# A Strassen-like down projection: places of the weight tiles, order of the first tile's parts, output additions, squares' sums

## The chip, the cores and the metric

One Trainium2 chip; the kernel runs on 1 core. The metric is the device time of that core in microseconds (us). The core has TensorE (PE, matmuls), VectorE (DVE), ScalarE (ACT), GpSimd (POOL) and SyncE (SP), which in this kernel issues all loads and stores; 16 DMA engines carry them out. The engines run each its own list of instructions in order and wait for each other on semaphores.

## The reference

One layer of a decoder, for 1024 prompt tokens and 64 sample tokens (1088 columns in the kernel), in float32. The change touches only its last lines:

```
    x = x + merged @ w_out
    h2 = rmsnorm(x, norm2_g)
    x = x + (jax.nn.silu(h2 @ w_gate) * (h2 @ w_up)) @ w_down
    return x, c_kv, k_r, v
...
    y_prompt = rmsnorm(xp, final_norm_g)
    y_sample = rmsnorm(xs, final_norm_g)
```

D_MODEL is 1024, D_FF 2816 (22 tiles of 128). Everything ahead of it (attention, gMLP, output projection) is the same instructions in both kernels.

## The kernel before

**Tiling.** Activations lie transposed: features on the 128 partitions, tokens along the free side. A product of a float32 operand pair is made of three matmuls of parts (`mm3`, L893 to L895): a *high* part, made by ACT as a rounded copy (L1474), and a *low* part, the rest, made by DVE as a subtraction. The MLP is not computed as one matmul: rows, columns and the sum index are each halved, and seven products of sums of the halves (M2, M6, M4, M1, M3, M5, M7 in this order) take the place of eight. `TURNS` is 11, `RING` is 4.

**Gate and up.** 11 turns of 7 products (j from 0 to 6, 6.0 us each on TensorE). ACT and POOL make the parts of the weights (`cw_hi`, `cw_lo`), DVE collects the results in `bufP`, `bufC` and `bufD` (L2442, semaphore `added`), ACT applies silu (L1805), DVE multiplies (`times`, L2489, semaphore `blocks`), and SP stores the four finished blocks in DRAM (`acts`, L592).

**Down.** 88 steps t: product p = t // 11, tile k = t % 11. In the first six products a step has 24 matmuls with 272 columns. The seventh (M7) is done in two halves of the columns, with 12 matmuls a step: t from `LAST` = 66 to 76, and from `LATE` = 77 to 87. For each step:

- SP (`load_down`) loads one or two blocks of `w_down` of 256 KB into place `t % RING` of `araw` (three blocks for M3, of which one goes to `a7` and stays for M7), and (`load_tile`) a tile of the activations into `ab[1]`, `ab[2]`, `ab[3]`. It also brings back the rows of x (`x<-x2s`). `load_down(t)` waits for the low part of the weights of tile t - 4, so SP follows DVE. `ab[0]` comes in two transfers (`load_ab0`): ten tiles in one (2720 KB), and the last tile alone.
- DVE sums the weight blocks (`down_sum`, L2567, L2571), sums the activation tiles (`act_sum`, L2584), and makes the low parts (`down_low`: `aHL` for the weights, L2592, and `bHL` for the activations, L2595). ACT makes the high parts (`down_high`, `act_high`) into rings of four.
- TensorE waits for `dn_lo` and adds into 8 PSUM banks. At a product's end ACT copies them to `part` (`keep_product`, at the third step of the next product, semaphore `dn_ev`), and DVE adds or subtracts `part` to one or two blocks of x2 (`add_parts`, L2605, at the fourth step, semaphore `y_add`). A block is 4 row tiles by half of the tokens. M7 goes from PSUM to x2 directly (`add_last`).

The order of DVE's instructions in one step t of the down projection is: `down_sum(t)`, `act_sum(t)`, `down_low(t - 1)`, then `add_parts`, then the extra work of the last steps.

**The last turn of gate and up** mixes both stages. The four places of `araw` are the same memory as the four places of `wraw` that hold gate and up weights. They come free in the order 0, 2, 3, 1 (`cw_lo` 1, 5, 6, 7 of the turn), and the loads of tile 0, 2, 3, 1 are issued at these points. `ab[0]` lies where operands of the first products lay, and is issued behind tile 3:

```
                sp_.wait_ge(cw_lo, PROD * i + 6)
                if last:
                    load_down(3)
                    load_ab0(0, TURNS - 1)
```

On ACT, `down_high(0)`, `act_high(0)` and `down_high(1)` stand behind `silu(i, bufC[:, 0, :], 11)`. On DVE, `down_sum(0)` and `down_sum(1)` stand ahead of the last additions (`block21`), `down_low(0)` stands between the second product of `bufC` and `block12`, `down_low(1)` behind `block12`.

**The final norm** is made for three groups of columns (`COLUMNS`: 544, 272, 272). ACT squares the blocks of x2 as they become final (`sqy`, `sqh`, `sqt`), DVE folds them (L2617, semaphore `n5_add`), TensorE sums over the partitions (`token_sums`, L1405), DVE makes means (L2624), POOL the power -1/2 (L885), DVE diagonals (L2632), TensorE spreads them over the partitions (`token_spread`, L1420), ACT copies that to `rs5`, and DVE scales (L1956). The first group's sums stand on TensorE ahead of step 73 (`LAST + 7`), its spread ahead of step 75 (`LAST + 9`); step 77 needs `rs5`. The folds of `sqy`, which belong to the second and third group, stand at step 70; those of `sqh` at 72 and 74.

Of the kernel before, what the change touches and what calls it, by code (L numbers as in the profile page):

```python
# [32 lines left out]
KD = D // P  # L33
# [56 lines left out]
           M3: ((1, 1), (3, 1)), M5: ((0, -1), (1, 1)), M7: ((0, 1),)}  # L90
STEPS = (PROD + 1) * TURNS
RING = 4
LAST, LATE = STEPS - 2 * TURNS, STEPS - TURNS
# [42 lines left out]
def build(nc, d):  # L136
    ctx = ExitStack()
    with ctx:
# [234 lines left out]
        ab_full = [sem(f"ab_full{b}") for b in range(4)]  # L373
        a_sum, b_sum, dn_hi, dn_lo = (sem(n) for n in ("a_sum", "b_sum", "dn_hi", "dn_lo"))
# [56 lines left out]
        def w_down(t):  # L431
            return a7[:, t % TURNS, :] if t >= LAST else araw[:, t % RING, 0, :]
# [39 lines left out]
        def _(sp_):  # L472
# [121 lines left out]
            def turn(i, last=False):  # L594
# [9 lines left out]
                if last:  # L604
                    load_down(2)
# [11 lines left out]
                if last:  # L617
                    load_down(1)
# [8 lines left out]
            def load_ab0(k0, k1):  # L627
# [4 lines left out]
                sp_.dma_start(ab[0][:, k0:k1, :], acts[0, k0:k1, :, :].rearrange("t p n -> p t n")).then_inc(ab_full[0], 16)  # L632
# [11 lines left out]
            def load_down(t):  # L644
# [3 lines left out]
                for x, (a, _) in enumerate(A_TERMS[p]):  # L648
                    sp_.dma_start(araw[:, t % RING, x, :], d["w_dn"][a, k, :, :]).then_inc(ff_full[t % RING], 16)
                if p == M3:  # L650
# [4 lines left out]
                    sp_.dma_start(a7[:, k, :], d["w_dn"][1, k, :, :]).then_inc(ff_full[t % RING], 16)  # L655
                    sp_.dma_start(araw[:, t % RING, 1, :], d["w_dn"][3, k, :, :]).then_inc(ff_full[t % RING], 16)
# [233 lines left out]
        def _(pe):  # L890
# [565 lines left out]
            pe.wait_ge(n5_add, 2)  # L1456
# [15 lines left out]
        def _(act):  # L1472
# [368 lines left out]
            def down_high(t):  # L1841
# [13 lines left out]
                else:  # L1855
                    act.wait_ge(ff_full[t % RING], raw_loads(t))
# [27 lines left out]
            def turn(i, par, last=False):  # L1884
# [8 lines left out]
                silu(i, bufC[:, 0, :], 11)  # L1893
# [4 lines left out]
                else:  # L1898
# [25 lines left out]
            for t in range(2, STEPS):  # L1924
# [12 lines left out]
                elif t == LAST + 5:  # L1937
                    act.wait_ge(y_add, adds_to(M7))
# [14 lines left out]
        def _(dve):  # L1953
# [581 lines left out]
            def turn(i, last=False):  # L2535
# [26 lines left out]
            def down_sum(t):  # L2562
                p, k = t // TURNS, t % TURNS
                if p < M7 and len(A_TERMS[p]) == 2:
                    dve.wait_ge(ff_full[t % RING], raw_loads(t))
                    x = araw[:, t % RING, :, :]
# [238 lines left out]
```

## Time and profile before

| | us |
|---|---|
| three timed runs | 1433.33, 1427.6, 1430.66; median 1430.66 |
| profiled execution: its time | 1435.15 |
| its span in the profile | 1433.4 |
| PE busy | 1345.6 (94%) |
| DVE busy | 834.2 (58%) |
| ACT busy | 507.9 (35%) |
| POOL busy | 427.5 (30%) |
| mean granted TensorE clock, of 2.4 GHz | 0.967 |

The page of the profile gives per engine the busy time, then the span in 40 slices, the chain of work that ended last (here 73% PE, 14% DVE), and the costliest groups of instructions. The costliest by far are the three matmul lines of the down projection (L893 to L895, 616 each, some 290 ns one). Matmuls overlap: one of 290 ns starts every 125 ns at the full clock. The down projection runs from 1168 us to 1420 us.

### The profile page before, as it was taken

Reading aid. Unit: us, or ns where it says so; the run is one execution under the profiler, and the core shown is the slowest. Engines: PE = TensorE matmul, PEld = TensorE weight load, DVE = VectorE, ACT = ScalarE, POOL = GpSimd, SP = SyncE. Lnnn points to the kernel's source line nnn. Section 1 sums busy time; section 2 is a strip of 40 time slices with the busy share of each in tenths; the row PEclk is TensorE's granted clock in tenths of the full one; section 3 lists DMA queues with packets and bytes.
Section 4 is the critical chain, followed back from the end, with each engine's and each line's share of the span. In section 5 each row is a group of like instructions: output and inputs, shape, how many; then the busy total and the mean of one; then the engine's idle time right before and its main releaser. Section 6 shows DMA issues by size and latency. Waiting matters only on the chain.

```text
span 1433.4 us, 23985 instructions
## 1 busy us (share of the span) xinstructions
PE 1345.6 (94%) x9450; PEld 1255.6 (88%) x9450; DVE 834.2 (58%) x1272; ACT 507.9 (35%) x884; POOL 427.5 (30%) x277
## 2 busy tenths in 40 slices
PE   6999997899999898999989999999999989999987
PEld 4778896788888765999989999999999989999987
DVE  4795035566665432717893444554344558989976
ACT  3413122565555422402432222222222224444451
POOL 1262232434433102566124444444444410000000
PEclk8999998899999799999999999999999999999998
DMA  7001000100005343463022212222222269857503
GB/s 237 17 30 64 31 30 12 65 1 19 1 16 176 137 138 121 165 211 102 27 83 84 81 61 75 75 82 75 82 74 77 76 226 327 285 191 237 168 1 125
DMA packets 66970, 146.33 MB, mean 102 GB/s; under 512 B 7778, under 2 KB 15330, under 8 KB 66178
## 3 DMA queue, kind: packets, MB, share of 16 engines
q1 hardware_dynamic: 66882, 145.12, 30.0%
q8 instruction: 59, 0.97, 0.3%
q14 instruction: 29, 0.24, 0.1%
HBM read 122.54 MB, written 22.55 MB: 101 GB/s over the span
## 4 chain that ended last, share of the span: by engine, by line
PE 73%; DVE 14%; issue 5%; DMA 3%; ACT 2%; POOL 1%; SPq 0%; DVEq 0%; POOLq 0%; ACTq 0%
PE ps L893 22%; PE ps L894 21%; PE ps L895 21%; DMA araw<-in_w_dn 2%; PE ps L1116 2%; PE ps L901 2%; DVE x L1956 2%; PE ps L1179 1%; DVE aHL L2592 1%; DMA x<-in_x 1%; DVE bHL L2595 1%; PE ps L1222 1%; DVE bsum L2584 1%; DVE uwL L2013 1%; DVE hL L2007 1%
## 5 line engine op out<-in xcount | busy, mean ns | idle before, releaser
L893 PE MATMUL ps<-bHL,aHL 128*128 128x272 f32 x616 | 179.9, 292 | 11.2 <-DVE bHL L2595 11.2
L862 POOL TENSOR_TENSOR ws<-wraw,ws 128x1024 fp32r<-128x1024 f32 x50 | 124.4, 2488 | 217.2 <-ACT ws L1474 217.2
L895 PE MATMUL ps<-bHL,aHL 128*128 128x272 f32 x616 | 179.1, 291 | 0.0
L894 PE MATMUL ps<-bHL,aHL 128*128 128x272 f32 x616 | 178.4, 290 | 0.0
L893 PEld LDWEIGHTS ps<-bHL,aHL 128*128 128x128 f32 x616 | 118.4, 192 | 12.8 <-DVE bHL L2595 12.7
L2442 DVE TENSOR_TENSOR bufP<-bufP,ps 128x544 f32<-128x544 f32 x66 | 47.4, 720 | 135.5 <-PE ps L895 133.2
L1474 ACT ACTIVATE ws<-wraw 128x1024 fp32r<-128x1024 f32 x55 | 58.4, 1061 | 173.5 <-PE ps L895 170.3
L895 PEld LDWEIGHTS ps<-bHL,aHL 128*128 128x128 f32 x616 | 117.9, 191 | 0.0
L894 PEld LDWEIGHTS ps<-bHL,aHL 128*128 128x128 f32 x616 | 117.7, 191 | 0.0
L2193 DVE TENSOR_TENSOR pTL<-ps,pTH 128x512 fp32r<-128x512 f32 (+1 forms) x96 | 53.1, 554 | 53.7 <-ACT pTH L1474 53.3
L885 POOL TENSOR_TENSOR rt<-ms,mhalf 128x3 f32<-128x3 f32 (+1 forms) x3 | 3.1, 1024 | 265.8 <-DVE ms L2624 265.8
L862 POOL TENSOR_TENSOR ws<-wsum,ws 128x1024 fp32r<-128x1024 f32 x20 | 58.3, 2913 | 61.8 <-ACT ws L1474 61.8
L808 POOL TENSOR_TENSOR prob<-prob,rsm 128x128 f32<-128x128 f32 (+5 forms) x48 | 49.6, 1041 | 88.5 <-DVE rsm L2168 88.5
L1474 ACT ACTIVATE aHL<-araw 128x512 fp32r<-128x512 f32 x66 | 41.6, 631 | 88.5 <-DVE araw L2567 58.0
L2442 DVE TENSOR_TENSOR bufC<-bufP,ps 128x544 f32<-128x544 f32 x42 | 30.2, 720 | 70.6 <-PE ps L895 70.6
L1474 ACT ACTIVATE pTH<-ps 128x512 fp32r<-128x512 f32 (+1 forms) x96 | 46.8, 489 | 51.4 <-PE ps L1116 50.6
L1116 PE MATMUL ps<-ident,prob 128*128 128x128 f32 x288 | 52.0, 287 | 10.7 <-DVE prob L2173 7.5
L1627 ACT ACTIVATE prob<-ps,nmx 128x128 f32<-128x128 f32 (+3 forms) x64 | 47.3, 740 | 23.2 <-DVE nmx L2179 23.2
L2179 DVE TENSOR_REDUCE nmx<-ps 128x1 f32<-128x128 f32 (+3 forms) x64 | 47.7, 750 | 12.2 <-PE ps L1097 12.1
L704 POOL TENSOR_TENSOR rt<-ms,mhalf 128x3 f32<-128x3 f32 x15 | 14.6, 976 | 134.0 <-DVE ms L1976 121.5
L893 PE MATMUL ps<-x6H,ws 128*128 128x272 f32 x176 | 51.7, 294 | 2.7 <-DVE x6L L2525 2.7
L1116 PEld LDWEIGHTS ps<-ident,prob 128*128 128x128 f32 x288 | 34.8, 146 | 19.9 <-DVE prob L2173 8.5
(362 smaller groups left out, 4640.1 us busy)
## 6 DMA issues: line engine op xcount, KB each, us to landing
araw<-in_w_dn SPq DMA_DIRECT2D x121, 256.0 KB, 3.3
wraw<-in_w_gu SPq DMA_DIRECT2D x44, 512.0 KB, 3.6
cp<-in_cache SPq DMA_DIRECT2D x64, 272.0 KB, 4.7
ab<-acts SPq DMA_DIRECT2D x34, 272.0 KB, 5.0
raw<-in_w_out SPq DMA_DIRECT2D x16, 512.0 KB, 4.4
acts<-bufC SPq DMA_DIRECT2D x22, 272.0 KB, 2.1
x<-in_x SPq DMA_DIRECT2D x4, 1088.0 KB, 7.4
x<-x2s SPq DMA_DIRECT2D x8, 544.0 KB, 6.6
```

The costliest lines, as they stand in the source:

```text
L808: pool.tensor_tensor(row, row, rsm[:, r % 4:r % 4 + 1].broadcast_to((P, n)), ALU.mult).then_inc(s_pn, 1)
L862: pool.tensor_tensor(w[:, 1, :], w_source(j), w[:, 0, :], ALU.subtract).then_inc(cw_lo, 1)
L893: nc.tensor.matmul(out, wh, xh, start=start, stop=False)
L894: nc.tensor.matmul(out, wh, xl, start=False, stop=False)
L895: return nc.tensor.matmul(out, wl, xh, start=False, stop=stop)
L901: last = nc.tensor.matmul(ps[:, bank, 0:n], ones[:, :], sq[:, kk, 0:n], start=kk == 0, stop=kk == k - 1)
L1116: last = nc.tensor.transpose(ps[:, 4 + x % 2, P * qi:P * qi + P], prob[:, at:at + P], ident[:, :])
L1474: return nc.scalar.activation(out, x, ACT.Copy, scale=scale)
L1627: nc.scalar.activation(prob[:, prob_at(qt):prob_at(qt) + n], psf[:, 1024 * (r % 2):1024 * (r % 2) + n], ACT.Exp, bias=nmx[:, s:s + 1], sca ...
L2179: nc.vector.tensor_reduce(nmx[:, s], psf[:, at:at + P * (qt + 1)], AX.X, ALU.max, negate=True).then_inc(s_nm, 1)
L2193: nc.vector.tensor_tensor(pTL[:, x % 4, c0:512], ps[:, 4 + x % 2, c0:512], pTH[:, x % 4, c0:512], ALU.subtract).then_inc(t_free, 1)
L2442: nc.vector.tensor_tensor(halves(out[:, g, :]), halves(x[:, g, :]), pair(b + 2 * g), ALU.add).then_inc(added, 1)
```

## The change

It reorders and renames; no product, load or matmul is added or taken away.

- **Places.** `SLOTS = (0, 2, 3, 1)`: tile t goes to place `SLOTS[t % 4]`. In the last turn tile 1 is loaded at the second of the four points, into place 2; tile 2 at the third, into place 3, behind the first part of `ab[0]`; tile 3 at the last, into place 1. The last tile of `ab[0]` has a semaphore of its own, `ab_last`.
- **First tile's parts.** On ACT, `down_high(0)`, `act_high(0)`, `down_high(1)` go ahead of the silu of `bufC`. On DVE, `down_low(0)` goes ahead of `block21`.
- **Additions apart.** `add_parts(p)`, which made one or two additions at the fourth step of the next product, becomes `add_part(p, x)`: the first at the fourth step, the second at the fifth. M5's targets change places, so block 1 is final first.
- **Squares' sums.** ACT squares block 1 at step 70 (was 71) after the first of M5's additions. DVE's `sqh` folds go from steps 72 and 74 to 71, 72 and 73; the `sqy` folds from step 70 to step 78, behind `token_diagonals(0)`. TensorE's waits on `n5_add` have new numbers.

```diff
-           M3: ((1, 1), (3, 1)), M5: ((0, -1), (1, 1)), M7: ((0, 1),)}
+           M3: ((1, 1), (3, 1)), M5: ((1, 1), (0, -1)), M7: ((0, 1),)}
...
+SLOTS = (0, 2, 3, 1)
...
-                engine.wait_ge(ab_full[0], 16 if k < TURNS - 1 else 32)
+                engine.wait_ge(ab_full[0] if k < TURNS - 1 else ab_last, 16)
...
-            return a7[:, t % TURNS, :] if t >= LAST else araw[:, t % RING, 0, :]
+            return a7[:, t % TURNS, :] if t >= LAST else araw[:, SLOTS[t % RING], 0, :]
...
                 sp_.wait_ge(cw_lo, PROD * i + 5)
                 if last:
-                    load_down(2)
+                    load_down(1)
...
                 sp_.wait_ge(cw_lo, PROD * i + 6)
                 if last:
-                    load_down(3)
                     load_ab0(0, TURNS - 1)
+                    load_down(2)
...
                 if last:
-                    load_down(1)
+                    load_down(3)
                     load_ab0(TURNS - 1, TURNS)
...
                 if t == LAST + 7:
-                    pe.wait_ge(n5_add, 6)
+                    pe.wait_ge(n5_add, 4)
...
-            pe.wait_ge(n5_add, 2)
+            pe.wait_ge(n5_add, 6)
...
-                silu(i, bufC[:, 0, :], 11)
                 if last:
                     down_high(0)
                     act_high(0)
                     down_high(1)
-                else:
+                silu(i, bufC[:, 0, :], 11)
+                if not last:
                     weights_high(i + 1, 0, 1 - par)
...
-                elif t == LAST + 5:
-                    act.wait_ge(y_add, adds_to(M7))
+                elif t == LAST + 4:
+                    act.wait_ge(y_add, adds_to(M5) + 1)
                     square(sqh[:, 0:KH, :], slice(0, KH), half1, n5_sq)
...
                     down_sum(0)
                     down_sum(1)
+                    down_low(0)
                 for g in range(2):
                     block21(i, g)
                 times(i, bufC, 3, 12)
-                if last:
-                    down_low(0)
...
-                if t % TURNS == RING - 1 and TURNS <= t < LATE:
-                    add_parts(t // TURNS - 1)
-                if t == LAST + 4:
-                    fold(sqy, 2, 1)
-                    dve.wait_ge(n5_add, 1)
-                    fold(sqy, 1, 1)
+                if TURNS <= t < LATE and t % TURNS in range(RING - 1, RING - 1 + len(TARGETS[t // TURNS - 1])):
+                    add_part(t // TURNS - 1, t % TURNS - RING + 1)
+                if t == LAST + 5:
+                    fold(sqh[:, KH:KD, :], 2, 2)
                 elif t == LAST + 6:
-                    fold(sqh[:, KH:KD, :], 2, 2)
-                elif t == LAST + 8:
                     fold(sqh[:, 0:KH, :], 2, 3)
-                    dve.wait_ge(n5_add, 4)
+                elif t == LAST + 7:
+                    dve.wait_ge(n5_add, 2)
                     nc.vector.tensor_tensor(sqh[:, 0:2, :], sqh[:, 0:2, :], sqh[:, KH:KH + 2, :],
                                             ALU.add).then_inc(n5_add, 1)
-                    dve.wait_ge(n5_add, 5)
+                    dve.wait_ge(n5_add, 3)
                     fold(sqh, 1, 3)
...
                 elif t == LATE + 1:
                     token_diagonals(0)
+                    fold(sqy, 2, 1)
+                    dve.wait_ge(n5_add, 5)
+                    fold(sqy, 1, 1)
```

SP's queue in the last turn, before (`araw<-in_w_dn` are weight blocks, two for a tile; `ab_173` is `ab[0]`):

```order
L592 DMA acts<-bufC 128x544
L649 DMA araw<-in_w_dn 128x512 x4
L632 DMA ab_173<-acts 128x10x544
L592 DMA acts<-bufD 128x544
L649 DMA araw<-in_w_dn 128x512 x2
L632 DMA ab_173<-acts 128x544
```

and now:

```order
L594 DMA acts<-bufC 128x544
L651 DMA araw<-in_w_dn 128x512 x2
L634 DMA ab_173<-acts 128x10x544
L651 DMA araw<-in_w_dn 128x512 x2
L594 DMA acts<-bufD 128x544
L651 DMA araw<-in_w_dn 128x512 x2
L634 DMA ab_173<-acts 128x544
```

The big transfer stands ahead of the third pair of blocks now, not behind it, and the pairs are those of tiles 1, 2, 3 instead of 2, 3, 1.

DVE in the same place, before (`aHL_183` and `bHL_177` are the parts of step 0, `aHL_184` and `bHL_178` of step 1):

```order
L2489 TENSOR_TENSOR bufD<-bufD 128x544
L2567 TENSOR_TENSOR araw<-araw 128x512 x2
L2442 TENSOR_TENSOR bufC<-bufC,ps 128x544 x2
L2489 TENSOR_TENSOR bufC<-bufC 128x544
L2592 TENSOR_TENSOR aHL_183<-araw,aHL_183 128x512
L2595 TENSOR_TENSOR bHL_177<-ab_173,bHL_177 128x544
L2442 TENSOR_TENSOR bufP<-bufP,ps 128x544 x2
```

and now:

```order
L2491 TENSOR_TENSOR bufD<-bufD 128x544
L2568 TENSOR_TENSOR araw<-araw 128x512 x2
L2593 TENSOR_TENSOR aHL_183<-araw,aHL_183 128x512
L2596 TENSOR_TENSOR bHL_177<-ab_173,bHL_177 128x544
L2444 TENSOR_TENSOR bufC<-bufC,ps 128x544 x2
L2491 TENSOR_TENSOR bufC<-bufC 128x544
L2444 TENSOR_TENSOR bufP<-bufP,ps 128x544 x2
```

Step 0's low parts moved ahead of the two additions into `bufC` and its product.

DVE in the last product, from the additions of M5 on, before (one `aHL` and one `bHL` row are a step's low parts, 69 first):

```order
L2605 TENSOR_TENSOR x_145<-x_145,part 128x4x544 x2
L2592 TENSOR_TENSOR aHL_184<-a_188,aHL_184 128x512
L2595 TENSOR_TENSOR bHL_178<-ab_174,bHL_178 128x272
L2617 TENSOR_TENSOR sqy<-sqy 128x1088
L2617 TENSOR_TENSOR sqy<-sqy 128x544
L2592 TENSOR_TENSOR aHL_194<-a_188,aHL_194 128x512
L2595 TENSOR_TENSOR bHL_179<-ab_174,bHL_179 128x272
L2592 TENSOR_TENSOR aHL_195<-a_188,aHL_195 128x512
L2595 TENSOR_TENSOR bHL_180<-ab_174,bHL_180 128x272
L2617 TENSOR_TENSOR sqh<-sqh 128x1088
```

and now:

```order
L2606 TENSOR_TENSOR x_145<-x_145,part 128x4x544
L2593 TENSOR_TENSOR aHL_184<-a_188,aHL_184 128x512
L2596 TENSOR_TENSOR bHL_178<-ab_174,bHL_178 128x272
L2606 TENSOR_TENSOR x_145<-x_145,part 128x4x544
L2593 TENSOR_TENSOR aHL_194<-a_188,aHL_194 128x512
L2596 TENSOR_TENSOR bHL_179<-ab_174,bHL_179 128x272
L2618 TENSOR_TENSOR sqh<-sqh 128x1088
L2593 TENSOR_TENSOR aHL_195<-a_188,aHL_195 128x512
L2596 TENSOR_TENSOR bHL_180<-ab_174,bHL_180 128x272
L2618 TENSOR_TENSOR sqh<-sqh 128x1088
```

The second addition stands behind step 69's low parts, the two `sqy` folds are gone from here, and each `sqh` fold comes a step or two earlier.

## Rows read from the trace of the kernel before

**Rows 1.** The page, busy time by engine: us, share, instructions

```profile
PE 1345.6 (94%) x9450; PEld 1255.6 (88%) x9450; DVE 834.2 (58%) x1272; ACT 507.9 (35%) x884; POOL 427.5 (30%) x277
```

**Rows 2.** Waits of TensorE, 1140 to 1434: waited for, us, times, longest

```profile
PE ps L893 <- DVE bHL L2595: 11.2, 7, 4.7
```

**Rows 3.** Timeline, the start: start, us, engine, line, [idle before <- releaser]

```profile
1150.27 0.39 SPq L632 DMA_DIRECT2D ab<-acts  x1
...
1164.40 0.69 DVE L2567 TENSOR_TENSOR araw<-araw 128x512 f32<-128x512 f32 x1 [7.46 <-DMA araw<-in_w_dn]
...
1166.84 0.64 ACT L1474 ACTIVATE bHL<-ab 128x544 fp32r<-128x544 f32 x1
...
1167.70 0.72 DVE L2595 TENSOR_TENSOR bHL<-ab,bHL 128x544 fp32r<-128x544 f32 x1
...
1168.47 0.60 PE L893 MATMUL ps<-bHL,aHL 128*128 128x272 f32 x1 [4.66 <-DVE bHL L2595]
...
1170.96 0.72 DVE L2489 TENSOR_TENSOR bufP<-bufP 128x544 f32<-128x544 f32 x1
...
1172.10 0.92 SPq L649 DMA_DIRECT2D araw<-in_w_dn  x2
```

**Rows 4.** The loads of `ab[0]`, line L632: time from issue to landing

```profile
DMA to landing us min/median/max: 7.0/8.9/10.9
```

**Rows 5.** Stretches: length, busy us of each engine (count), PEclk, DMA share, GB/s

```profile
1164.00:1168.40 4.40, 0.00 (x0) 0.00 (x0) 3.90 (x7) 2.24 (x4) 0.00 (x0) 0.87 0.08 34
1168.40:1174.00 5.60, 5.53 (x24) 5.53 (x25) 5.40 (x10) 2.83 (x6) 0.00 (x0) 0.50 0.26 94
1186.00:1192.00 6.00, 6.00 (x50) 6.00 (x49) 4.22 (x7) 2.36 (x4) 0.00 (x0) 1.00 1.05 401
1377.00:1382.00 5.00, 1.92 (x14) 1.55 (x12) 4.96 (x7) 4.38 (x8) 0.00 (x0) 1.00 0.00 0
1390.00:1394.00 4.00, 4.00 (x19) 4.00 (x20) 2.46 (x7) 0.00 (x0) 1.17 (x1) 0.50 0.00 0
```

**Rows 6.** Timeline, first product: step 1, two low parts, eviction, step 11

```profile
1174.08 0.29 PE L893 MATMUL ps<-bHL,aHL 128*128 128x272 f32 x1
...
1177.11 0.72 DVE L2595 TENSOR_TENSOR bHL<-ab,bHL 128x544 fp32r<-128x544 f32 x1
...
1180.47 0.72 DVE L2595 TENSOR_TENSOR bHL<-ab,bHL 128x544 fp32r<-128x544 f32 x1
...
1204.76 2.15 ACT L1474 ACTIVATE part<-ps 128x544 f32<-128x544 f32 x4
...
1205.51 0.36 PE L893 MATMUL ps<-bHL,aHL 128*128 128x272 f32 x1 [1.40 <-DVE bHL L2595]
```

**Rows 7.** Timeline: the first pair of additions, steps 14 and 47 on TensorE

```profile
1207.80 4.97 DVE L2605 TENSOR_TENSOR x<-x,part 128x2176 f32<-128x2176 f32 x2
...
1215.30 0.39 PE L893 MATMUL ps<-bHL,aHL 128*128 128x272 f32 x1 [0.59 <-DVE bHL L2595]
...
1315.62 0.39 PE L893 MATMUL ps<-bHL,aHL 128*128 128x272 f32 x1 [0.59 <-DVE bHL L2595]
```

**Rows 8.** Timeline, last product: additions, step 69, fold, token sums, power, diagonals, spread

```profile
1373.33 4.99 DVE L2605 TENSOR_TENSOR x<-x,part 128x2176 f32<-128x2176 f32 x2 [1.94 <-ACT part L1474]
...
1379.32 0.39 PE L893 MATMUL ps<-bHL,aHL 128*128 128x272 f32 x1 [2.16 <-DVE bHL L2595]
...
1386.16 1.28 DVE L2617 TENSOR_TENSOR sqh<-sqh 128x1088 f32<-128x1088 f32 x1
...
1389.58 2.29 PE L1405 MATMUL ps<-ones,sqh 128*128 128x1 f32 x10 [2.47 <-DVE sqh L2617]
...
1392.54 1.17 POOL L885 TENSOR_TENSOR rt<-ms,mhalf 128x5 f32<-128x5 f32 x1 [237.17 <-DVE ms L2624]
...
1395.66 0.82 DVE L2632 TENSOR_TENSOR diag<-ident,rt 128x640 f32<-128x640 f32 x1
...
1396.70 1.85 PE L1420 MATMUL ps<-diag,ones 128*128 128x128 f32 x16
```

More of the change, by code:

```diff
@@ L373, in build @@
         ab_full = [sem(f"ab_full{b}") for b in range(4)]
+        ab_last = sem("ab_last")
         a_sum, b_sum, dn_hi, dn_lo = (sem(n) for n in ("a_sum", "b_sum", "dn_hi", "dn_lo"))
@@ L631, in load_ab0 @@
                 sp_.wait_ge(act_out[0], 16 * k1)
-                sp_.dma_start(ab[0][:, k0:k1, :], acts[0, k0:k1, :, :].rearrange("t p n -> p t n")).then_inc(ab_full[0], 16)
+                sp_.dma_start(ab[0][:, k0:k1, :], acts[0, k0:k1, :, :].rearrange("t p n -> p t n")).then_inc(ab_full[0] if k0 == 0 else ab_last, 16)
             def load_tile(b, k):
@@ L654, in load_down @@
                         sp_.wait_ge(dn_lo, 2 * TURNS * M1)
-                    sp_.dma_start(a7[:, k, :], d["w_dn"][1, k, :, :]).then_inc(ff_full[t % RING], 16)
-                    sp_.dma_start(araw[:, t % RING, 1, :], d["w_dn"][3, k, :, :]).then_inc(ff_full[t % RING], 16)
+                    sp_.dma_start(a7[:, k, :], d["w_dn"][1, k, :, :]).then_inc(ff_full[SLOTS[t % RING]], 16)
+                    sp_.dma_start(araw[:, SLOTS[t % RING], 1, :], d["w_dn"][3, k, :, :]).then_inc(ff_full[SLOTS[t % RING]], 16)
             turn(0)
@@ L1855, in down_high @@
                 else:
-                    act.wait_ge(ff_full[t % RING], raw_loads(t))
+                    act.wait_ge(ff_full[SLOTS[t % RING]], raw_loads(t))
                 hi(weights_of(t)[:, 0, :], w_down(t)).then_inc(dn_hi, 1)
@@ L2564, in down_sum @@
                 if p < M7 and len(A_TERMS[p]) == 2:
-                    dve.wait_ge(ff_full[t % RING], raw_loads(t))
-                    x = araw[:, t % RING, :, :]
+                    dve.wait_ge(ff_full[SLOTS[t % RING]], raw_loads(t))
+                    x = araw[:, SLOTS[t % RING], :, :]
                     nc.vector.tensor_tensor(x[:, 0, :], x[:, 0, :], x[:, 1, :],
@@ L2569, in down_sum @@
                 elif p == M3:
-                    dve.wait_ge(ff_full[t % RING], raw_loads(t))
-                    nc.vector.tensor_tensor(a7[:, k, :], a7[:, k, :], araw[:, t % RING, 1, :],
+                    dve.wait_ge(ff_full[SLOTS[t % RING]], raw_loads(t))
+                    nc.vector.tensor_tensor(a7[:, k, :], a7[:, k, :], araw[:, SLOTS[t % RING], 1, :],
                                             ALU.subtract).then_inc(a_sum, 1)
@@ L2595, in down_low, with add_part @@
                 nc.vector.tensor_tensor(x[:, 1, :], act_of(t), x[:, 0, :], ALU.subtract).then_inc(dn_lo, 1)
-            def add_parts(p):
+            def add_part(p, x):
+                b, sign = TARGETS[p][x]
                 dve.wait_ge(dn_ev, KH * (p + 1))
-                for x, (b, sign) in enumerate(TARGETS[p]):
-                    for j in range(2):
-                        dve.wait_ge(ld_x[2 * (b // 2) + j], 64)
-                    if adds_to(p) + x:
-                        dve.wait_ge(y_add, adds_to(p) + x)
-                    nc.vector.tensor_tensor(y_block(b), y_block(b), part[:, :, :],
-                                            ALU.add if sign > 0 else ALU.subtract).then_inc(y_add, 1)
+                for j in range(2):
+                    dve.wait_ge(ld_x[2 * (b // 2) + j], 64)
+                if adds_to(p) + x:
+                    dve.wait_ge(y_add, adds_to(p) + x)
+                nc.vector.tensor_tensor(y_block(b), y_block(b), part[:, :, :],
+                                        ALU.add if sign > 0 else ALU.subtract).then_inc(y_add, 1)
             with dve.Fori(0, (TURNS - 3) // 2) as i:
```

2 lines of the change are left out of this document (1 added, 1 removed).

## The prediction

> **What bounds the kernel now.** I first read the page's engine lines: TensorE's matmuls are busy for 94% of the span [rows 1], so only places where TensorE stops, or runs at its lower clock, can give time. Next, the waits of TensorE in the down projection [rows 2]: 11.2 us in 7 waits, all for DVE's L2595, the low part of an activation operand. The timeline says where they lie and which of them the change touches. A *step* below is one tile t of the down projection; step t cannot start before `down_low(t)` has made both low parts. A full step takes 2.99 us at the full clock, a step of the last product (t from 66 on) 1.5 us (24 and 12 matmuls of about 0.125 us).
>
> Three places count. (a) Step 0 starts at 1168.47 after 4.66 us of idleness, that is, the gate and up stage ended at 1163.8 [rows 3]. Then the granted clock is 0.50, the 1.2 GHz level, until step 1 begins at 1174.08 [rows 5, 6]: 5.6 us instead of 3.0. (b) Steps 14 and 47 start 0.59 us late each, behind DVE's pairs of output additions [rows 7]. (c) In the last product step 69 starts 2.16 us late, step 70 again late, the token sums 2.47 us late and then at the lower clock [rows 5, 8].
>
> **Place a: the start.** DVE sat 7.46 us in `down_sum(1)` until the second tile's two weight blocks landed, at 1164.40 [rows 3]. Those are issued last of the first four tiles, behind the 2720 KB load of `ab[0]`. With the change tile 1 goes to the place that tile 2 had, two gate and up products (12 us) earlier; the 7.46 us go. What is late next? `down_low(0)` needs `ab[0]`, issued at 1150.27 and landed 10.9 us later, at 1161.2 [rows 3, 4]. The new order issues it ahead of two 256 KB blocks instead of behind them: 0.85 us earlier (two issues), and with 0.52 MB less ahead of it, 1.3 us at the 401 GB/s of [rows 5]. So it lands between 1159.0 (both) and 1161.2 (neither). I take 1160.0.
>
> Here one rule of the Trainium skill bears on the choice. "DMA: Bandwidth & Descriptors", under "Queues, rings and completion order", says that each DMA engine takes descriptors in ring order, while completion is not first in, first out. By the first half alone the landing would be 1159.0, by the second it could stay at 1161.2. No row here shows a transfer of this size behind another and also ahead of it.
>
> From a landing at 1160.0 the rest is a chain of known pieces: ACT's high part 0.64, DVE's low part 0.72, two bufC additions, the product, two bufP additions, again low part and product, each of 128x544 and 0.72 or less like the rows of [rows 3], with ACT's silus, of the size of a high part, beside or between them. It has `down_low(0)` ready at 1161.4, before TensorE is free at 1163.8, so step 0 starts at 1163.85, without idleness and without the lower clock. Step 1 is ready at 1166.2 (wanted at 1166.85), the last product of the block (row 1170.96 of [rows 3]) ends at 1166.9, and SP, whose next tile load is queued behind that product's store, issues `load_down(4)` at 1167.35 instead of 1172.10: 4.75 us earlier. With the landing at 1161.2 it is 3.55; with 1159.0, where the last gate and up matmul at 1163.8 becomes the limit, 5.15.
>
> Now the important cut. TensorE would be 7.2 us earlier at step 1 (1174.08 to 1166.85), but it doesn't keep that. In the first product the weight blocks, the `ab[1]` tiles and the returning rows of x keep the DMA engines full: 401 GB/s [rows 5], and `down_low(4)` followed `down_low(3)` by 3.36 us (1177.11 to 1180.47, [rows 6]), not by 2.99. Before, TensorE's late and slow step 0 covered that: `down_low(3)` ended at 1177.83 and step 3 was wanted only at 1180.06 (1174.08 and two steps). Now the feed moves by 4.75 and TensorE by 7.2, so steps 3 to 7 wait 0.2 to 0.5 us each. At step 11 the feed sets the time already: ACT evicts the first product only after `act_high(13)`, at 1204.76, and step 11 starts at 1205.51 [rows 6]. That whole chain moves with SP's first issue. **Term a: 4.75 us (3.55 to 5.15; 7.2 if the feed should catch up).**
>
> **Place b: additions apart.** Two additions of 2.45 us each (4.97 together) sit between `down_low(13)` and `down_low(14)` [rows 7]. Apart, the second goes behind `down_low(14)`: step 14 loses its 0.59 us and the start-up 0.1; `down_low(15)`, behind both, ends as before, about 0.1 us later than TensorE now wants it. Gain 0.6. At step 47 the same pattern gives 0.6 (there `down_low(48)` becomes 0.15 late). The pairs at steps 36 and 58 held nobody up and are worth nothing; DVE's total work there is unchanged, so the short wait at step 44, whose low parts come late by a wait of SP's, stays. **Term b: 1.2 us (0.7 to 1.5).**
>
> **Place c: the last product.** DVE's additions start at 1373.33, TensorE ends step 68 at 1377.15 [rows 8]. In the new order: addition 1 ends at 1375.8, step 69's low parts at 1376.8 (they take 1.0 us: 1378.32 to 1379.32), in time; 2.16 us saved. Addition 2 to 1379.2, step 70 ready at 1380.15 (1.6 late), fold 1.28 us and low parts: step 71 ready at 1382.3 (0.6 late), fold and low parts: step 72 at 1384.4 (0.6 late), the joining addition 1.28 and the half-size fold 0.7: token sums at 1386.4 instead of 1389.58. Taking the sqy folds, 2.0 us, out ahead of the sums is part of this. Gain so far 3.2. ACT's square of block 1 comes 2 us earlier in its queue, ahead of the highs of step 71; those end at 1379.7 and are wanted at 1381.3, so they cost nothing. The ten matmuls of the sums ran at the 0.50 clock [rows 5]; at the full clock they take 1.15 instead of 2.29. Then comes a part that gives something back: the mean is read by DVE only after the low parts of steps 73 to 76 (4 by 0.95: 1390.1; before, the sums themselves came last), the power takes 1.17 us on POOL, the diagonals 0.82, and the spread before step 75 starts at 1392.45 instead of 1396.70 [rows 8], after some 1.9 us of idleness. The sqy folds now follow the diagonals; TensorE has steps 75 and 76 in stock and DVE is through at 1394.4, 2.8 us before the first addition from step 76 needs it: free. Everything behind (second token sums, last scaling, stores of y) hangs on TensorE's end and moves along. **Term c: 4.25 us (2.3 if the lower clock is no part of a usual execution, up to 4.6).**
>
> The semaphore `ab_last`, one more DVE instruction per pair and the sign order of M5 cost nothing that a row shows: they lie on engines with idle time there.
>
> **Sum.** 4.75 + 1.2 + 4.25 = 10.2 us. The profiled execution took 1435.15 us, so it would take 1424.95. It lies 4.5 us above the median of the three runs; I take the difference off the median: 1430.66 - 10.2 = 1420.5.
>
> **Rivals.**
> 1. *The lower clock was a thing of the profiled execution.* TensorE idled 3.1 of the 5.0 us from 1377 to 1382 and stayed at the full clock, and lost it some 5 us later, after 2.47 idle us [rows 5, 8]. If the timed executions mostly keep it, the sums' 1.15 and step 73's 1.36 us weren't there to win: term c about 2.2, the time 1422.5. Speaks for it: the timed runs are all faster than the profiled one.
> 2. *The feed doesn't move.* If the DMA engines deliver the first product's tiles no earlier (a slower stretch, or `ab[0]` 1 to 2 us later than 1161.2), term a falls to 0 to 1.5 and the time is about 1425.5. Against it: they are nearly idle from 1164 to 1174, 34 and 94 GB/s [rows 5], and only SP's wait keeps them so.
> 3. *New waits lower the clock.* The idle stretches are 1.6, 0.6, 0.6, 0.4 and 1.9 us in the last product, and one drop there costs about 2.6 us: 1423.
> 4. *Slower than before.* The mechanism is the same clock in the starved steps 3 to 7: a step at the lower level costs 2.6 us more (5.61 against 2.99). Four such steps eat the whole gain; seven, with the half steps of the last product at 1.36 each, make it slower by over 0.5%, about 1439. Against it: these waits are under 0.5 us of each 3.4, and 3.1 idle us of 5.0 left the clock at 1.00 [rows 5].
>
> The Trainium skill's rule speaks for 3 and 4: "TensorE: Matmul & The Clock Gate" holds the slow level for the default which activity releases, and its section "HAM oscillation" describes loops whose DMA waits bring it back each time. The trace agrees at 1168.4 (0.50 after 4.66 us idle) and disagrees at 1377 to 1382.
>
> **Chances.** My sum 0.56, rival 1 0.16, rival 2 0.11, rival 3 0.10, rival 4 0.04, a head start kept in full (7.2, about 1418) 0.03. A measurement of this kernel tells about 0.5% (7.2 us, a time below 1423.5) from no change. Faster by more: nearly all of the sum's case, most of rival 1, half of 3: 0.76; within: 0.18; slower: 0.06. The sum's own ends, 6.6 to 11.3 us, give 1419.4 to 1424.1 and three runs of before lie 5.7 us apart; with most of the rivals inside, the range is 1415.5 to 1426.5.
>
> **What would show it.** Right: DVE's second `down_sum` runs at once behind the first; no wait of over 0.3 us before step 0, and no stretch at 0.50 there; SP's first load after the bufP store about 4 to 5 us earlier; short waits before steps 3 to 7 and about 2 us before step 11; steps 14 and 47 without 0.6 us waits; token sums some 3.2 us earlier against step 66, the spread some 4.2. Wrong: an `ab[0]` landing past 1161.7, which delays step 0 one for one; DMA rates under 380 GB/s in the first product; a clock of 0.50 anywhere past 1160.

## The result, and the profile after

| | before | changed |
|---|---|---|
| median of 6 runs, us | 1430.56 | 1422.88 |
| lowest and highest | 1427.6, 1434.26 | 1418.28, 1424.3 |
| profiled execution: time, span | 1435.15, 1433.4 | 1424.3, 1422.6 |

The ratio of the runs is 0.9937, with a 95% interval of 0.9917 to 0.9957; the medians lie 7.7 us apart. This ratio, here and below, is not the quotient of the two medians (that would be 0.9946); where the two disagree by a microsecond or two, the scatter of the runs is that large. One execution of the kernel before in the last set of runs took 4572 us and is left out of every ratio. The prediction was 1420.5 with a range from 1415.5 to 1426.5. A second set of six runs of the changed kernel, in the experiments below, gave 0.9943 (0.9920 to 0.9965).

The page of the changed kernel, busy time by engine, and then TensorE's waits from 1140 us on; before, they were 11.2 us in 7 waits [rows 1, 2]:

```profile
PE 1342.5 (94%) x9450; PEld 1251.7 (88%) x9450; DVE 834.3 (59%) x1272; ACT 508.4 (36%) x884; POOL 427.9 (30%) x277
```

```profile
PE ps L895 <- DVE bHL L2596: 5.0, 6, 1.7
```

The timeline of the start (to be read against [rows 3]; columns: start, us, engine, line, instruction, and in brackets the idle time before it and who ended it):

```profile
1146.65 0.39 SPq L634 DMA_DIRECT2D ab<-acts  x1
...
1153.54 1.28 DVE L2568 TENSOR_TENSOR araw<-araw 128x512 f32<-128x512 f32 x2
...
1156.78 0.66 ACT L1476 ACTIVATE bHL<-ab 128x544 fp32r<-128x544 f32 x1 [1.81 <-DMA ab<-acts]
...
1157.47 0.72 DVE L2596 TENSOR_TENSOR bHL<-ab,bHL 128x544 fp32r<-128x544 f32 x1 [1.78 <-ACT bHL L1476]
...
1160.93 0.29 PE L895 MATMUL ps<-bHL,aHL 128*128 128x272 f32 x1
...
1163.01 0.71 DVE L2491 TENSOR_TENSOR bufP<-bufP 128x544 f32<-128x544 f32 x1
...
1164.13 0.92 SPq L651 DMA_DIRECT2D araw<-in_w_dn  x2
```

DVE makes both weight sums at once. What is late next is `ab[0]`, as the prediction said, but with room: step 0's low parts are ready at 1158.2, and TensorE goes from the last gate and up matmul to step 0 at 1160.93 without a pause.

The profiled executions reach that point at different times (1163.82 before, 1161.09 here; 1158.1 to 1166.1 over all profiles of this study), although TensorE's instructions ahead of it are the same. So times below are counted from the **end of gate and up** (start of its last matmul and 0.29 us), which takes this scatter out. For each profile they are the starts of TensorE's steps:

| us | before | changed | gain by then |
|---|---|---|---|
| step 0 | 4.65 | -0.16 | 4.8 |
| step 11 | 41.69 | 35.86 | 5.8 |
| step 15 | 54.58 | 47.90 | 6.7 |
| step 44 | 142.01 | 135.63 | 6.4 |
| step 48 | 154.89 | 147.67 | 7.2 |
| step 66 | 208.65 | 201.54 | 7.1 |
| step 75 | 234.58 | 224.32 | 10.3 |
| step 77 | 237.70 | 229.54 | 8.2 |
| step 87 | 254.27 | 246.19 | 8.1 |

Of the spans' difference, 10.8 us, 8.1 come from the down projection and 2.7 from ahead of it, where TensorE's instructions are the same and which scatters by 8 us over the profiles. The table also shows where something was given back: 2.1 us between steps 75 and 77. Stretches of the changed kernel (length, busy us and count of PE, PEld, DVE, ACT, POOL, then TensorE's granted clock as a share of 2.4 GHz, DMA share, GB/s; compare [rows 5]):

```profile
1160.00:1165.00 5.00, 5.00 (x42) 5.00 (x41) 4.72 (x8) 1.79 (x4) 0.00 (x0) 1.00 0.25 96
1176.00:1182.00 6.00, 5.80 (x45) 5.42 (x44) 3.02 (x6) 1.52 (x4) 0.00 (x0) 1.00 1.05 409
1380.60:1382.60 2.00, 0.28 (x3) 0.06 (x2) 0.94 (x3) 0.43 (x1) 1.09 (x1) 1.00 0.00 0
1382.60:1385.40 2.80, 2.80 (x16) 2.80 (x17) 2.22 (x3) 0.00 (x0) 0.00 (x0) 0.63 0.00 0
1385.40:1388.30 2.90, 2.90 (x14) 2.90 (x15) 0.00 (x0) 0.69 (x2) 0.00 (x0) 0.50 0.00 0
```

The clock is 1.00 at the start now. But it falls to 0.63 and then 0.50, the 1.2 GHz level, during the spread of the first columns' norm and steps 75 and 76. The timeline of TensorE's late starts in the last product, with the power and the diagonals that the spread waits for (see [rows 8]):

```profile
1370.20 0.39 PE L895 MATMUL ps<-bHL,aHL 128*128 128x272 f32 x1 [1.45 <-DVE bHL L2596]
...
1376.48 1.28 PE L1407 MATMUL ps<-ones,sqh 128*128 128x1 f32 x10 [0.20 <-DVE sqh L2618]
...
1380.39 1.29 POOL L887 TENSOR_TENSOR rt<-ms,mhalf 128x5 f32<-128x5 f32 x1 [227.75 <-DVE ms L2625]
...
1381.72 0.83 DVE L2633 TENSOR_TENSOR diag<-ident,rt 128x640 f32<-128x640 f32 x1 [1.06 <-POOL rt L887]
...
1382.60 2.98 PE L1422 MATMUL ps<-diag,ones 128*128 128x128 f32 x16 [1.72 <-DVE diag L2633]
```

And in the first product, ACT's eviction and step 11 (see [rows 6]):

```profile
1196.20 2.15 ACT L1476 ACTIVATE part<-ps 128x544 f32<-128x544 f32 x4
...
1196.95 0.36 PE L895 MATMUL ps<-bHL,aHL 128*128 128x272 f32 x1 [1.71 <-DVE bHL L2596]
```

### The profile page after: what moved, and what is told of

The parts are those of the page before. It is cut to its first block, busy times and chain, and to the rows that moved or that the text cites. A ratio compares the mean times of both kernels' runs of the same rounds, so it can differ in the third digit from the quotient of the medians.

```text
span 1422.6 us, 23990 instructions
## 1 busy us (share of the span) xinstructions
PE 1342.5 (94%) x9450; PEld 1251.7 (88%) x9450; DVE 834.3 (59%) x1272; ACT 508.4 (36%) x884; POOL 427.9 (30%) x277
## 4 chain that ended last, share of the span: by engine, by line
PE 75%; DVE 13%; issue 5%; DMA 3%; ACT 2%; POOL 1%; SPq 0%; POOLq 0%; DVEq 0%; ACTq 0%
PE ps L895 22%; PE ps L896 22%; PE ps L897 22%; PE ps L1118 2%; PE ps L903 2%; DMA araw<-in_w_dn 2%; DVE x L1958 1%; PE ps L1181 1%; DVE aHL L2593 1%; DVE bHL L2596 1%; PE ps L1224 1%; DVE uwL L2015 1%; DVE hL L2009 1%; PE ps L911 1%; DMA raw<-in_w_out 1%
## 5 line engine op out<-in xcount | busy, mean ns | idle before, releaser
L1476 ACT ACTIVATE aHL<-araw 128x512 fp32r<-128x512 f32 x66 | 41.6, 631 | 89.5 <-DVE araw L2568 62.5
L1118 PEld LDWEIGHTS ps<-ident,prob 128*128 128x128 f32 x288 | 35.8, 150 | 19.9 <-DVE prob L2175 8.5
```

The lines of the kernel that those rows point to most:

```text
L1118: last = nc.tensor.transpose(ps[:, 4 + x % 2, P * qi:P * qi + P], prob[:, at:at + P], ident[:, :])
L1476: return nc.scalar.activation(out, x, ACT.Copy, scale=scale)
```

## The experiments

My theory after the result: three independent gains, from the start (5.8 us), from the additions (1.7 us) and from the last product (3 to 4 us up to the spread), of which the last is eaten in part by a fall of the clock behind a new idle stretch of 1.7 us. The rivals are named with each run. "Before" was run beside each set. All ratios are against it.

**The start alone.** The kernel before with the places, the loads' order and the first tile's parts:

```diff
+SLOTS = (0, 2, 3, 1)
...
-                    load_down(3)
                     load_ab0(0, TURNS - 1)
+                    load_down(2)
...
-                silu(i, bufC[:, 0, :], 11)
                 if last:
                     down_high(0)
                     act_high(0)
                     down_high(1)
...
+                silu(i, bufC[:, 0, :], 11)
...
                     down_sum(1)
+                    down_low(0)
                 for g in range(2):
                     block21(i, g)
```

> The kernel before with the start alone changed: places of the tiles, order of the loads, first tile's parts ahead. My theory: the profile after shows step 11 at 36.0 us behind the end of gate and up, against 41.7 before; so this alone saves 5.7 us (about 1424.9 beside a before of 1430.6). Rival 'feed doesn't move in usual executions': 0 to 2 us. In the profile: no clock of 0.50 at step 0, short waits before steps 5 to 7, 1.7 us before step 11, and steps 14 and 47 still 0.6 us late.

Measured: 1424.76 us against 1430.84, ratio 0.9948 (0.9928 to 0.9969), 6.1 us between the medians. Step 11 is at 36.25, step 14 is still 0.57 us late.

**The places and loads alone**, with ACT's and DVE's order as before:

```diff
+SLOTS = (0, 2, 3, 1)
...
-                    load_down(2)
+                    load_down(1)
...
-                    load_down(3)
                     load_ab0(0, TURNS - 1)
+                    load_down(2)
...
-                    load_down(1)
+                    load_down(3)
```

> The kernel before with the places and the order of the loads alone; ACT's and DVE's order at the start as before. Theory 'the seven idle microseconds of DVE behind the second tile were all of it, and the ready time of ab[0] leaves room': the first low parts end some 2.8 us ahead of the end of gate and up even in the old order, so step 0 doesn't wait and all of the start's gain, 5.5 to 6 us, is there (about 1425). Rival 'the first tile's parts ahead of the last blocks are needed': step 0 late by 1 us or more and less than 4.5 us saved.

Measured: 1424.6 us against 1430.89, ratio 0.9957 (0.9941 to 0.9973), 6.3 us. Step 0 doesn't wait, step 11 is at 35.19. The whole gain of the start is here, and the order adds nothing: with it, step 11 was at 36.25.

**The order alone**, with the old places and loads:

```diff
-                silu(i, bufC[:, 0, :], 11)
                 if last:
                     down_high(0)
                     act_high(0)
                     down_high(1)
...
+                silu(i, bufC[:, 0, :], 11)
...
                     down_sum(1)
+                    down_low(0)
                 for g in range(2):
                     block21(i, g)
                 times(i, bufC, 3, 12)
-                if last:
-                    down_low(0)
```

> The kernel before with the order at the start alone: first tile's high parts ahead of the silu on ACT, first low parts ahead of the last additions on DVE, old places and loads (and a semaphore of its own for the last tile of ab[0]). Theory 'DVE's wait for the second tile is the cause': that wait of some 7.5 us stays, step 0 comes about 2 us earlier (2.6 instead of 4.6 us late) since its parts are made first, but SP's next loads don't, so step 11 is where it was, 41 to 42 us behind the end of gate and up: 0 us (about 1430.8). Rival 'the order is a part of the gain': 1 us or more at step 11.

Measured: 1433.02 us against 1432.11, ratio 1.0002 (0.9983 to 1.002). Step 11 is at 42.37, no earlier than before. I missed on step 0, which I had put at 2.6 us: it is 4.61 us late as it was, for another reason. DVE's and TensorE's rows:

```profile
1165.93 0.69 DVE L2567 TENSOR_TENSOR araw<-araw 128x512 f32<-128x512 f32 x1 [8.77 <-DMA araw<-in_w_dn]
...
1168.63 0.57 PE L894 MATMUL ps<-bHL,aHL 128*128 128x272 f32 x1 [4.61 <-DVE bufC L2443]
```

The wait for the second tile stands (8.77 us here) and, since `down_sum(1)` stands ahead of `down_low(0)`, it holds the low parts too. Behind them come the `bufC` additions, which TensorE now waits for. The order merely chooses which of the two TensorE waits for.

**`ab[0]` behind tile 2** in the changed kernel:

```diff
-                    load_ab0(0, TURNS - 1)
                     load_down(2)
+                    load_ab0(0, TURNS - 1)
```

> The changed kernel with the ten tiles of ab[0] loaded behind tile 2's two blocks and not ahead of them. Theory 'the engines take the transfers in the order of issue': ab[0] lands 1.5 to 2.2 us later, some 2.6 us ahead of the end of gate and up instead of 4.3; step 0 still doesn't wait, SP's first load comes 0.5 to 1.5 us later and step 11 with it: 1 us slower than the changed kernel. Rival 'it lands no later': no difference at all.

Measured: 1425.89 us, beside the changed kernel's own 1424.14 in the same set; ratio to before 0.9954 (0.9933 to 0.9976). The medians' 1.75 us are within the scatter, the profile is clearer: `ab[0]` takes 11.7 us from issue to landing, against 10.1 in the first profile of the changed kernel, and lands at -1.8 (1163.34 against an end of gate and up at 1165.17) instead of -4.4 (1156.70 against 1161.09). The same split runs through all 14 profiles: with the big transfer ahead of the third pair of blocks it takes 9.3 to 10.1 us (nine profiles), behind them 10.9 to 13.4 us (five). Tile 2's two blocks show it too: they land 2.6 and 2.9 us after their issue in this run, and 10.1 and 11.4 us in the changed kernel, where the big transfer stands ahead of them. Step 11 is at 37.85 instead of 36.16 in that set. Against the expectation, step 0 does wait, 0.45 us, and waits again inside:

```profile
1165.62 0.36 PE L895 MATMUL ps<-bHL,aHL 128*128 128x272 f32 x1 [0.45 <-DVE bufC L2444]
...
1167.62 0.39 PE L895 MATMUL ps<-bHL,aHL 128*128 128x272 f32 x1 [0.26 <-DVE bufP L2444]
```

So these transfers are served in the order of issue. The landing moved by 2.6 us and step 0 by 0.6 (from -0.16 to 0.45): the start had about 2 us of room, and by step 3 the whole 2.4 us are lost.

**The additions apart, without the last product**:

```diff
-            def add_parts(p):
+            def add_part(p, x):
...
+                if TURNS <= t < LATE and (t < LAST) and t % TURNS in range(RING - 1, RING - 1 + len(TARGETS[t // TURNS - 1])):
+                    add_part(t // TURNS - 1, t % TURNS - RING + 1)
+                elif t % TURNS == RING - 1 and TURNS <= t < LATE and not (t < LAST):
+                    for x in range(len(TARGETS[t // TURNS - 1])):
+                        add_part(t // TURNS - 1, x)
```

> The kernel before with the additions apart in the products before the last one alone. My theory: 1.4 us saved (the two waits of 0.59 us and their start-up), which five rounds can hardly tell from nothing; the profile must show steps 14 and 47 without a wait, and nothing new at steps 36, 37, 58, 59. Rival: the waits only move one step on, 0 us.

Measured: 1429.04 us against 1430.84, ratio 0.9980 (0.9966 to 0.9994), 1.8 us between the medians. Steps 11 to 15 take 12.04 us instead of 12.89, and so do steps 44 to 48; no new wait at 36, 37, 58 or 59.

**The last product alone**: M5's additions apart and in the other order, squares and folds at the new steps.

```diff
-                elif t == LAST + 5:
-                    act.wait_ge(y_add, adds_to(M7))
+                elif t == LAST + 4:
+                    act.wait_ge(y_add, adds_to(M5) + 1)
...
-                if t == LAST + 4:
-                    fold(sqy, 2, 1)
...
                 elif t == LATE + 1:
                     token_diagonals(0)
+                    fold(sqy, 2, 1)
```

> The kernel before with the last product alone changed (M5's additions apart and in the other order, squares and folds at new steps). My theory from the profile after: 3.2 us are won up to step 75, and 2.2 to 3.2 are given back, since TensorE now idles 1.7 us ahead of the spread and the clock falls to 0.50 there for the spread and steps 75 and 76: saved in all about 1.0 us. Rival (my prediction's term c): 4.25 us. The profile's clock between the spread and step 77 tells them apart.

Measured: 1429.84 us against 1430.84, ratio 0.9986 (0.9973 to 0.9999), 1.0 us between the medians (2.0 by the ratio). The size is the one that I expected, but the profile disagrees with the mechanism that I gave for it: the same 1.72 us of idleness stand ahead of the spread, and the clock doesn't fall. From step 66 to 77 it takes 24.89 us (before: 29.05; changed kernel: 28.00). Its spread and the stretch behind it:

```profile
1391.45 1.96 PE L1420 MATMUL ps<-diag,ones 128*128 128x128 f32 x16 [1.72 <-DVE diag L2632]
```

```profile
1393.20:1396.20 3.00, 3.00 (x25) 3.00 (x25) 1.19 (x4) 1.12 (x3) 0.00 (x0) 1.00 0.00 0
```

**The changed kernel once more.**

> The changed kernel itself once more, beside these. Theory 'the fall of the clock ahead of the spread hangs on how the waits fall against the chip's own time, not on the code': with the same waits of 1.45, 0.39, 0.40, 0.20 and 1.7 us, step 77 lies 24.9 or 28.0 us behind step 66, either being possible. Rival 'it belongs to the changed kernel': 28.0 again. The median 1421.5 to 1423.5.

Measured: 1424.14 us against 1432.11, ratio 0.9943 (0.9920 to 0.9965), 0.6 us above the range that I had given, and a profile without the fall of the clock:

```profile
1386.57 1.96 PE L1422 MATMUL ps<-diag,ones 128*128 128x128 f32 x16 [1.75 <-DVE diag L2633]
```

Step 77 is 24.85 us behind step 66. Together with the run above and those below there are five profiles with this last product: three without the fall (24.89, 24.86, 24.85) and two with it (28.00 and 27.98). All five have waits of 1.4, 0.4, 0.4, 0.2 and 1.7 us in the same places. The five profiles with the old last product have 29.05, 27.69, 27.09, 27.65 and 27.69, each with a fall somewhere between steps 70 and 74: at the sums in the kernel before, already at step 70 in the one with the additions apart, where a stretch reads

```profile
1380.50:1386.00 5.50, 5.50 (x25) 5.50 (x26) 5.46 (x9) 1.28 (x3) 0.00 (x0) 0.52 0.00 0
```

and at step 73, behind sums of 1.27 to 1.28 us at the full clock, in the other three. Why the same waits sometimes cost the clock and sometimes not stays open.

**The spread one step later** in the changed kernel:

```diff
-                elif t == LAST + 9:
+                elif t == LAST + 10:
                     token_spread(0, (5, 7))
```

> The changed kernel with the spread of the first columns' norm on TensorE one step later, behind step 75 instead of ahead of it. Theory 'the idle stretch ahead of the spread costs the clock': step 75 (1.5 us) fills the stretch, 0.3 us of idleness stay, the clock stays at 1.00, the spread takes 1.85 us or less instead of 2.98 and steps 75 to 76 3.1 instead of 5.2: 4 to 5 us faster than the changed kernel (about 1418.5). Rival 'the clock falls from the sum of the waits at steps 70 to 73, whatever stands ahead of the spread': only the 1.4 us of idleness are saved and the stretch at 0.50 stays (about 1421.5).

Measured: 1418.89 us against 1430.84, ratio 0.9914 (0.9888 to 0.994). That is 4.0 us below the changed kernel's first median, and 5.3 below its second, but those medians come from other sets, and the intervals of the ratios (0.9888 to 0.9940 here, 0.9917 to 0.9957 there) overlap: the timed runs alone don't show the gain. In the profile, step 75 fills the stretch:

```profile
1388.04 1.96 PE L1422 MATMUL ps<-diag,ones 128*128 128x128 f32 x16 [0.20 <-DVE diag L2633]
```

Steps 66 to 77 take 23.38 us: 1.5 us less than the changed kernel without the fall, 4.6 less than with it. The 1.5 us are shown. That the filled stretch also protects the clock is not: this profile and the three below that keep the late spread have no fall, but neither have three of the five profiles with the stretch open.

**Means and diagonals earlier as well:**

```diff
-                elif t == LATE:
+                elif t == LAST + 9:
                     token_means(0)
-                elif t == LATE + 1:
+                elif t == LATE:
                     token_diagonals(0)
+                elif t == LATE + 1:
                     fold(sqy, 2, 1)
```

> The previous experiment's late spread, with DVE's means at step 75 and diagonals at step 77 instead of 77 and 78. Theory: the diagonals are ready before step 75 ends, the last 0.2 us wait ahead of the spread goes, 0.3 to 0.5 us beside the late spread alone (about 1418.4) and no stretch at 0.50 behind the sums. Rival 'the clock falls from the waits at steps 70 to 72': the stretch appears before the sums or behind them in part of the executions all the same.

Measured: 1418.17 us against 1430.89, ratio 0.9914 (0.9892 to 0.9935). Steps 66 to 77 take 22.91 us, 0.47 less; no wait and no fall behind the sums.

**And M5's second addition later:**

```diff
-                if TURNS <= t < LATE and t % TURNS in range(RING - 1, RING - 1 + len(TARGETS[t // TURNS - 1])):
+                if TURNS <= t < LATE and t % TURNS in range(RING - 1, RING - 1 + len(TARGETS[t // TURNS - 1])) and t != LAST + 4:
                     add_part(t // TURNS - 1, t % TURNS - RING + 1)
...
                     token_diagonals(0)
+                    add_part(M5, 1)
```

> The same with M5's second addition (2.45 us of DVE, block 0, which nobody needs before step 76's results are added) at step 77 instead of 70. Theory 'DVE sets steps 70 to 72 and the sums': step 70 loses its 1.45 us wait, the sums come 1.5 to 1.9 us earlier, step 80 may wait 0.3 us; 1.3 to 1.7 us faster than with early means alone (about 1417). Rival: DVE is late again at steps 78 to 80 and gives it all back.

Measured: 1416.91 us against 1430.89, ratio 0.9896 (0.9871 to 0.9921). Steps 66 to 77 take 21.14 us, 1.8 less: step 70 starts without a wait. Behind it 0.55 us are given back, steps 77 to 87 take 17.12 instead of 16.57.

**The early rows of x three steps later** in the changed kernel:

```diff
-            rows_back = {2 * j + 1 + (0 if m >= KH else TURNS): m for m in range(KD) for j in (m % KH,)}
+            rows_back = {2 * j + 4 + (0 if m >= KH else TURNS): m for m in range(KD) for j in (m % KH,)}
```

> The changed kernel with the four early returning rows of x loaded three steps later each (behind steps 4, 6, 8, 10 instead of 1, 3, 5, 7). Theory 'the DMA engines' rate sets the feed of the first product': with 1.1 MB out of the way of tiles 5 to 9 the waits of 0.2 to 0.4 us before steps 5 to 7 go, and with one row of 0.56 MB behind tile 13, step 11 comes 1 to 1.4 us earlier; 1 to 1.5 us faster than the changed kernel. Rival 'the chain of DVE, SP and the time to landing sets it': steps 5 to 7 and 11 as before, 0 us.

Measured: 1419.75 us against 1430.89, ratio 0.9926 (0.9905 to 0.9948); beside the changed kernel, 3.1 us at the first median. Step 11 is at 33.72 us instead of 35.86, the waits before steps 5 to 7 are gone (as they are in two other profiles with the rows in their old place, so that sign proves nothing), and step 11's is

```profile
1191.81 0.37 PE L895 MATMUL ps<-bHL,aHL 128*128 128x272 f32 x1 [0.56 <-DVE bHL L2596]
```

It takes out 2.1 us where I expected 1.0 to 1.4. Step 11 was at 33.7 and 33.8 in the two profiles with later rows and at 35.2 to 36.3 in the seven with the rows and `ab[0]` in the changed kernel's places, so the rows do hold step 11 back. Whether by the DMA engines' load or by the 0.4 to 0.5 us that SP spends on each issue is not separated, and the size stays unexplained.

**All of it together**: late spread, early means, late second addition, rows later.

> The changed kernel with the late spread, the early means, the late second addition and the rows of x three steps later. Theory: the two sets of gains lie at different places and add up: step 11 at 33.7 us behind the end of gate and up, step 77 at 21.1 us behind step 66, about 7 us less than the changed kernel, some 1415.5. Rival 'they share the slack of DVE': less than 5 us together.

Measured: 1417.55 us against 1432.11, ratio 0.9896 (0.9873 to 0.992), 6.6 us below the changed kernel in the same set, 2 us above the 1415.5 that I expected. Step 11 is at 33.79, step 77 is 21.15 us behind step 66: in the profile both gains are whole, 2.1 and 3.7 us. In time it can't be told from the version before it without the later rows (the same ratio, 0.9896): both beat the changed kernel, which of the two is better stays open. Its profiled execution reached the end of gate and up at 1166.12, the latest of all.

## Why the prediction was right, point by point

**Place a, mechanism right, size 4.75 predicted, 5.8 measured.** DVE's idle time behind the second tile went, `ab[0]` was late next, and its landing (10.1 us after an issue at 1146.65, that is -4.4 us, and -4.4 to -5.1 over the nine profiles with this order; my 1160.0 was -3.8) left step 0 alone. SP's first load came 5.24 us earlier against the end of gate and up (8.28 to 3.04), for 4.75 predicted. I had set the upper end of 5.15 by TensorE's last gate and up matmul; it was reached, and all nine profiles have it within 0.01 us (3.04 or 3.05). The cut of the 7.2 us came as said: steps 5, 6 and 7 wait by 0.2 to 0.5 us, step 11 by 1.71, at 409 GB/s. The run with the later rows shows that the returning rows of x are a part of it. That rests on the profiles; over four profiles with the old start step 11 is at 41.1 to 42.4, over seven with the new one and the rows in place at 35.2 to 36.3 (means 41.6 and 35.8).

**What I gave credit to wrongly in place a** is the order on ACT and DVE. I let it share the gain without pricing it; the places alone bring 6.3 us and the order alone none. With `ab[0]` early, it is worth nothing that these runs can show.

**Place b, 1.2 predicted, 1.7 measured** (0.85 at each place): I had left 0.1 to 0.15 us of lateness at steps 15 and 48 that didn't come. One wrong number in the prediction: the wait at step 44 does not stay constant. It was 0.66 and is 0.84 here, and lies between 0.3 and 1.75 in the other profiles, with nothing changed near it.

**Place c, 4.25 predicted, 1.1 in the profile.** This is the term that was mis-sized. One of the signs that I had named for being wrong, a clock of 0.50 past 1160, did appear. Up to the start of the spread every term was right: against step 66 the sums came 3.26 us earlier (3.2 predicted) and the spread 4.26 (4.25 predicted), ahead of it 1.72 us idle (1.9 predicted). What I missed is that this idle stretch can cost the clock: the spread took 2.98 us instead of 1.85 and steps 75 and 76 took 5.22 instead of 3.12. That was rival 3, price 2.6 us and time 1423, with a chance of 0.10; measured were 1422.88 us. But the other profiles show that it isn't always so, and rival 1 is in there too: the lower clock is a part of every profile of the old last product, though it cost 1.4 to 2.0 us less in four of the five than in the one that I worked from (27.1 to 27.7 us against 29.05). By mean over the profiles, the old one takes 27.8 us from step 66 to 77, the new one 26.1. So term c is worth about 1.7 us, from few profiles that scatter by 2 and 3 us, and the last product alone measured 1.0 at the medians (0.1 to 3.9 by its interval). In the one old profile with the full clock from the sums on (the additions apart) the spread came 22.16 us behind step 66, held by the diagonals, against 19.97 in the new one: 2.2 us, the figure of rival 1. The exact share of executions with the fall stays open; the timed runs don't tell the clock by place.

**Luck in the total.** Places a and b gave 1.0 and 0.5 us more than their terms, place c 3.2 less; the errors cancel in part. That the time came within 2.4 us of 1420.5 is no proof of the terms, and which clock the timed executions had at the spread is not known.

**The Trainium skill.** The rule of "DMA: Bandwidth & Descriptors" on ring order ("Queues, rings and completion order") is borne out for these transfers: with two blocks of 256 KB put ahead of it and issued 0.9 us later, the 2720 KB transfer took 11.7 us instead of 10.1, and 10.9 to 13.4 instead of 9.3 to 10.1 over all profiles. The means of the two groups, 12.2 and 9.7 us, lie 2.5 us apart; the 1.3 us that I had worked out from 401 GB/s were too few. "TensorE: Matmul & The Clock Gate", "HAM oscillation", warns of clock losses that come back with each idle stretch. The traces agree only in part: the 1.7 us stretch lost the clock in two profiles of five. Filling the stretch brought 1.5 us of idleness back; that it also saves the clock, as the section would have it, these runs are too few to show.

**The rivals.** The feed did move, so rival 2 fell. The starved steps kept the clock at 1.00 in all ten profiles of the changed start, so rival 4 fell. Even the run with `ab[0]` behind tile 2, where the waits of 0.45, 0.26 and 0.23 us come on top at steps 0 and 1, kept it there.

**The gains don't add exactly.** Parts a, b and c alone gave 6.1 (or 6.3), 1.8 and 1.0 us, 8.9 to 9.1 together, against 7.7 and, in the second set, 8.0 for all. By the ratios it is 0.86% against 0.63% and 0.57%. The intervals, 2 to 3 us each way for each ratio, cover that.

## What to carry to other kernels

When several loads are issued as places come free, give the first place to what is used first, and count the time until a queue's *next* load as well: here DVE's wait for one tile also put back SP's next loads by 5 us. A gain on TensorE is only kept as far as the feed behind it moves too, so work out the next limit (here the arrival of the first product's tiles) before adding up. And when a step is split or moved, look for the small stretch in which TensorE now has nothing: moving one instruction group by one step (the spread) took out 1.5 us in the profile, about what the whole of the last product's change is worth (1.0 at the medians, 1.7 over the profiles). And compare several profiles before giving a fall of the clock a price.

## What the hardware showed that I had not expected

- The same idle pattern, to 0.1 us, lost TensorE's full clock in two profiles (0.50 for some 7 us, from the spread on) and kept it in three, at a price of 3.1 us between steps 66 and 77. Before, 3.1 idle us of 5.0 had kept it [rows 5].
- Up to the end of gate and up TensorE has the same instructions in all 14 profiles, and reaches it between 1158.1 and 1166.1 us. The mean granted clock up to there goes with it only in part: 0.98 in the earliest (1158.09), 0.97 both in the latest (1166.12) and in the one at 1160.49. The rest of the cause stays open; anything under a few us has to be read from a fixed point in the profile, not from the total.
- The load of the ten tiles of `ab[0]`, in the same place in SP's queue, 0.5 us behind a pair of weight blocks, took 10.9, 11.7, 12.2, 12.7 and 13.4 us in five profiles: where a step hangs on one such landing, one profile gives its time to within 2.5 us only.
